# MLP input tiles and attention value rows transposed in 32x32 blocks on VectorE, regrouped through DRAM

## The reference

```
h = rmsnorm(x);  q, k, v, u, qx, gates = split(h @ w_in)
y_attn = windows of 128 keys over chunks of 64, 8 query heads, 2 kv heads of 64, with sinks
y_ssm  = glu(gelu(state space layer(u)));  y_mem = cross attention(qx, 256 memory rows)
merged = sum over branches of sigmoid(gate) * (y @ w_branch)
x = x + rmsnorm(merged @ w_out)
h2 = rmsnorm(x);  out = x + rmsnorm(relu(h2 @ w_up)**2 @ w_down)
```

## Time and profile before

| | |
|---|---|
| median of 3 runs | 1439.28 us (1438.74 to 1439.55) |
| profiled execution, its own time | 1438.89 us |
| its span, first to last instruction | 1436.9 us |
| mean granted clock | 0.998 |
| PE / PE weight load / DVE / ACT / POOL busy | 99% / 82% / 73% / 36% / 17% |
| PE's part of the chain that ended last | 94% |
| DMA | 227 MB, 158 GB/s over the span |

### The profile page before, as it was taken

One profiled execution on the slowest core, in us unless ns is written; L12 is line 12 of the kernel. 1 busy time (PEld: TensorE's weight loads), 2 busy tenths in 40 slices (PEclk: granted clock), 3 DMA queues, 4 the chain that ended last, 5 costly groups with the idle time before them and its releaser, 6 DMA issues.

```text
span 1436.9 us, 18375 instructions
## 1 busy us (share of the span) xinstructions
PE 1422.6 (99%) x6998; PEld 1178.1 (82%) x6998; DVE 1047.4 (73%) x1718; ACT 514.9 (36%) x637; POOL 241.7 (17%) x392
## 2 busy tenths in 40 slices
PE   8999999999999999999999999999999999999997
PEld 7888688878888888888888888888888888888886
DVE  6769768964854526456766779797979796979887
ACT  4445653131211352311333432333334333434334
POOL 0003313431111131001000304211010102020112
PEclk9999999999999999999999999999999999999999
DMA  9306525954234387234433447936363737364546
GB/s 337 74 30 190 166 85 175 275 195 149 71 106 139 93 272 256 93 96 151 162 104 89 133 146 228 299 118 203 119 203 117 234 94 239 105 203 143 160 152 117
DMA packets 136241, 227.04 MB, mean 158 GB/s; under 512 B 23048, under 2 KB 74288, under 8 KB 136176
## 3 DMA queue, kind: packets, MB, share of 16 engines
q0 software_dynamic: 52960, 139.24, 31.2%
q1 hardware_dynamic: 83200, 86.92, 19.1%
q10 hardware_dynamic: 16, 0.00, 0.0%
HBM read 175.53 MB, written 50.59 MB: 157 GB/s over the span
## 4 chain that ended last, share of the span: by engine, by line
PE 94%; DVE 3%; DMA 1%; issue 1%; ACT 0%; DVEq 0%; SPq 0%; ACTq 0%
PE bank L2146 55%; PE bank L2515 17%; PE bank L2535 15%; PE bank L2186 1%; PE bank L2156 1%; PE bank L2248 1%; PE bank L2268 1%; DMA raw<-in_w_down_dram 1%; PE bank L2375 1%; PE bank L2380 1%; PE bank L2284 1%; PE bank L2345 1%; PE bank L2330 1%; DMA xst<-in_mem_dram 0%; DVE wlo L388 0%
## 5 line engine op out<-in xcount | busy, mean ns | idle before, releaser
L2146 PE MATMUL bank<-hThi,whi 128*128 128x512 f32 x800 | 313.9, 392 | 0.1
L2146 PE MATMUL bank<-hThi,wlo 128*128 128x512 f32 x800 | 311.4, 389 | 0.0
L2146 PE MATMUL bank<-hTlo,whi 128*128 128x512 f32 x800 | 311.4, 389 | 0.0
L2146 PEld LDWEIGHTS bank<-hThi,whi 128*128 128x128 f32 x800 | 150.2, 188 | 32.2 <-issue 1.2
L2146 PEld LDWEIGHTS bank<-hThi,wlo 128*128 128x128 f32 x800 | 150.2, 188 | 31.6
L2146 PEld LDWEIGHTS bank<-hTlo,whi 128*128 128x128 f32 x800 | 150.2, 188 | 30.7
L1212 ACT ACTIVATE whi<-raw 128x1024 fp32r<-128x1024 f32 x91 | 95.3, 1055 | 182.3 <-DVE raw L1953 97.6
L1943 DVE TENSOR_TENSOR wlo<-raw,whi 128x1024 fp32r<-128x1024 f32 x91 | 110.9, 1219 | 34.4 <-ACT whi L1212 34.4
L2535 PE MATMUL bank<-whi,yhi 128*128 128x512 f32 x336 | 130.8, 389 | 0.6 <-DVE acc L1976 0.6
L2535 PE MATMUL bank<-wlo,yhi 128*128 128x512 f32 x336 | 130.7, 389 | 0.0
L2515 PE MATMUL bank<-hThi,whi 128*128 128x512 f32 x336 | 130.7, 389 | 0.0
(11 more groups left out here) (398 smaller groups left out, 2568.7 us busy)
## 6 DMA issues: line engine op xcount, KB each, us to landing
hThi<-h_scratch POOLq DMA_DIRECT2D x42, 512.0 KB, 4.8
hTlo<-h_scratch POOLq DMA_DIRECT2D x42, 512.0 KB, 5.7
raw<-in_w_in_dram SPq DMA_DIRECT2D x34, 512.0 KB, 7.2
raw<-in_w_up_dram SPq DMA_DIRECT2D x32, 512.0 KB, 4.3
raw<-in_w_down_dram SPq DMA_DIRECT2D x32, 512.0 KB, 4.6
gate_scratch<-scr POOLq DMA_DIRECT2D x48, 256.0 KB, 3.1
tok<-gate_scratch POOLq DMA_DIRECT2D x24, 512.0 KB, 4.2
prob_scratch<-pT POOLq DMA_DIRECT2D x16, 512.0 KB, 3.5
```

The costliest lines, as they stand in the source:

```text
L2146: ins = T.matmul(dst, lhs(k)[p], rhs(k)[q], start=start and k == 0 and i == 0, stop=stop and k == kt - 1 and i == 2)
```

## The change

- Attention: stage `vwin` is gone from PE and ACT. DVE transposes vT in 32x32 blocks right after `rope(7)`; POOL stores the result and, after the first gate unit, loads it back in four DMAs as `vwin` [128, 4, 16, 32]. `spv` issues 8 products of 256 columns per pair of chunks instead of 4, each 32 output channels wide, in four column groups.
- Output stage: for tiles 0 to 5, DVE transposes h2 in 32x32 blocks into acc[:, t] right after making it; POOL stores that (512 KB), waits for the store, and loads it back regrouped in four DMAs (128 KB each) over the same slot of `tok`. ACT and DVE make the high and low part from that slot in place of a bank. PE's 8 transposes per tile are gone for these tiles; before the MLP it waits for DVE's count of low parts. Tiles 6 and 7 stay as they were.
- `vwin` took 4 bank uses and h0 to h5 took 12, 16 in all, so the banks of all later uses are unchanged.

```
-OUT_ORDER stages: ("vwin", 4), ("out", 28)
+                  ("out", 16)
+HB = 6
...
+h2_slot = lambda t: tok[:, (2 + t % 2) * D:(3 + t % 2) * D]
+v_dram = nc.dram_tensor("v_blocks_scratch", (P, 2, NCH, 32), f32, kind="Internal").ap()
+hb_dram = nc.dram_tensor("h2_blocks_scratch", (HB, P, L), f32, kind="Internal").ap()
...
 # POOL, attention
+pool.wait_ge(blocks_turned, 9)
+g.dma_start(v_dram.rearrange("p b m r -> p (b m r)"), blocks[:, 0, :]).then_inc(blocks_out[0], 16)
 gates_out(0)
+pool.wait_ge(rope_done, 10)
+pool.wait_ge(blocks_out[0], 80)
+for b in range(4):
+    src = v_dram[:, b % 2, b // 2:b // 2 + 15, :].rearrange("(a s) m r -> s a (m r)", a=4)
+    g.dma_start(vwin[32 * b:32 * b + 32, :, 1:NCH, :].rearrange("s a m r -> s a (m r)"), src).then_inc(p_back, 16)
...
 # POOL, output stage, per tile t, behind the load of x
                     x_load(t + 2)
+                if t < HB:
+                    pool.wait_ge(blocks_turned, 17 + t + 1)
+                    g.dma_start(hb_dram[t], acc[:, t, :]).then_inc(blocks_out[t % 2], 16)
+                    pool.wait_ge(blocks_out[t % 2], 128 + 16 * (1 - t % 2) + 16 * (t // 2 + 1))
+                    src = hb_dram[t].rearrange("(a s) (b x) -> b s a x", a=4, b=4)
+                    for b in range(4):
+                        g.dma_start(h2_slot(t)[32 * b:32 * b + 32, :].rearrange("s (a x) -> s a x", a=4), src[b]).then_inc(xp_back[t % 2], 16)
...
 # ACT
-            for e in range(4):
-                copy_out(FIRST["vwin"] + e, vwin[:, 4 * e:4 * e + 4, :].rearrange("p n d -> p (n d)"))
...
             def h2_hi(t):
+                if t < HB:
+                    act.wait_ge(xp_back[t % 2], 16 * 16 + 64 * (t // 2 + 1))
+                    for e in range(2):
+                        A.activation(hThi[:, 4 * e:4 * e + 4, t * P:(t + 1) * P].rearrange("p k (a r) -> p k a r", a=4),
+                                     h2_slot(t).rearrange("p (a k r) -> p k a r", a=4, k=KT)[:, 4 * e:4 * e + 4], ACT.Copy).then_inc(split_hi, 1)
+                    return
...
 # DVE, after rope(7)
+            dve.wait_ge(blocks_out[0], 64)
+            V.transpose(blocks[:, 0, :].rearrange("p (b m r) -> p m b r", b=2, m=NCH),
+                        vT[:, :].rearrange("p (m b s) -> p m b s", m=NCH, b=2)).then_inc(blocks_turned, 1)
...
 # DVE, residual(t) and h2(t)
+                if 4 <= t < HB + 4:
+                    dve.wait_ge(blocks_out[t % 2], 128 + 16 * (1 - t % 2) + 16 * (t // 2 - 1))
...
+                if t < HB:
+                    dve.wait_ge(h2_made, t + 1)
+                    V.transpose(acc[:, t, :].rearrange("p (b k r) -> p k b r", b=4, k=KT),
+                                h2_slot(t).rearrange("p (k b s) -> p k b s", k=KT, b=4)).then_inc(blocks_turned, 1)
...
 # DVE, h2_lo(t)
+                if t < HB:
+                    for e in range(2):
+                        by_block = lambda y: y[:, 4 * e:4 * e + 4, t * P:(t + 1) * P].rearrange("p k (a r) -> p k a r", a=4)
+                        dve.wait_ge(split_hi, 20 + 2 * t + e + 1)
+                        V.tensor_tensor(by_block(hTlo), h2_slot(t).rearrange("p (a k r) -> p k a r", a=4, k=KT)[:, 4 * e:4 * e + 4],
+                                        by_block(hThi).bitcast(f32), sub).then_inc(h_parts, 1)
+                    return
...
 # PE
-            for e in range(4):
-                starts = [max(0, 64 * (4 * e + i - 1)) for i in range(4)]
-                transposes(FIRST["vwin"] + e, [vT[:, s0:s0 + P] for s0 in starts])
...
-                    for j in range(2):
-                        t0 = 4 * j + 2 * nn
+                    for a4 in (0, 2, 1, 3):
+                        t0 = 4 * (a4 // 2) + 2 * nn
...
                 if step[0] == "h":
-                    h2_transposes(t)
+                    if t >= HB:
+                        h2_transposes(t)
...
-            for t in range(4):
-                for e in range(2):
-                    wait_taken(pe, out_event("h", t, e))
+            pe.wait_ge(h_parts, 8)
```

More of the change, by code:

```diff
@@ L42 @@
 U_GATE = [9, 12, 13] + list(range(14, 23))
-STAGES = [("front", 26), ("qx", 12), ("spar", 1), ("xsc", 16), ("q", 8), ("kv", 4), ("xpv", 8), ("ssc0", 8), ("g0", 4), ("vwin", 4),
[1 row of a table removed]
+STAGES = [("front", 26), ("qx", 12), ("spar", 1), ("xsc", 16), ("q", 8), ("kv", 4), ("xpv", 8), ("ssc0", 8), ("g0", 4),           ("ssc1", 8), ("u", 8), ("g1", 4), ("g2", 4), ("spc", 2), ("spv", 8), ("s5a0", 2), ("g3", 4),
           ("s5m0", 2), ("g4", 4), ("s5y0", 2), ("s5a1", 2), ("g5", 4), ("s5m1", 2), ("g6", 4), ("s5y1", 2), ("s5a2", 2),
           ("g7", 4), ("s5m2", 2), ("g8", 4), ("s5y2", 2), ("s5a3", 2), ("g9", 4), ("s5m3", 2), ("g10", 4), ("s5y3", 2), ("g11", 4), ("mergeA", 16),
-          ("glu", 16), ("mergeM", 16), ("mergeS", 16), ("out", 28), ("upA", 4), ("mlp", 192)]
+          ("glu", 16), ("mergeM", 16), ("mergeS", 16), ("out", 16), ("upA", 4), ("mlp", 192)]
 OUT_ORDER = ["w0", "w1", "w2", "h0", "w3", "h1", "w4", "h2", "w5", "h3", "w6", "h4", "w7", "h5", "h6", "h7"]
+HB = 6
+OUT_EVENTS = [w for w in OUT_ORDER if w[0] == "w" or int(w[1]) >= HB]
 FIRST = {}
@@ L136, in out_event @@
         return FIRST["upA"] + 2 + 3 * (t - 6) + e
-    return FIRST["out"] + 2 * OUT_ORDER.index(f"{kind}{t}") + e
+    return FIRST["out"] + 2 * OUT_EVENTS.index(f"{kind}{t}") + e
 UP_FIRST = [(0, 0, 0), (0, 1, 0), (1, 0, 0), (1, 1, 0), (0, 0, 1), (0, 1, 1), (1, 0, 1), (1, 1, 1)]
@@ L228, in hybrid_layer @@
                 with overlay() as ov2:
-                    vwin = ov2("vwin", [P, NCH, P])
+                    vwin = ov2("vwin", [P, 4, NCH, 32])
         with overlay() as ov:
@@ L315, in hybrid_layer @@
         x_turned, x_out, x_back_in = sem("x_turned"), sem("x_out"), sem("x_back_in")
+        h_parts = sem("h_parts")
         blocks_turned, blocks_out, p_back = sem("blocks_turned"), [sem(f"blocks_out{s}") for s in range(2)], sem("p_back")
@@ L708, in blocks_back @@
             def blocks_back(q):
[L710 removed]
+                pool.wait_ge(blocks_out[q % 2], 64 + 16 * (1 - q % 2) + 16 * (q // 2 + 1))
                 src = p_dram[q].rearrange("(a s) (b x) -> b s a x", a=4, b=4)
@@ L715, in _ @@
             for q in range(8):
-                pool.wait_ge(blocks_turned, 8 + q + 1)
+                pool.wait_ge(blocks_turned, 9 + q + 1)
                 g.dma_start(p_dram[q], blocks[:, q % 2, :]).then_inc(blocks_out[q % 2], 16)
@@ L1546, in _ @@
             rope(7)
+            for e in range(2, 4):
+                wait_taken(dve, FIRST["kv"] + e)
+            dve.wait_ge(blocks_out[0], 64)
+            V.transpose(blocks[:, 0, :].rearrange("p (b m r) -> p m b r", b=2, m=NCH),
+                        vT[:, :].rearrange("p (m b s) -> p m b s", m=NCH, b=2)).then_inc(blocks_turned, 1)
             SS = float(HD) ** -0.5
@@ L1651, in _ @@
             for h in range(2):
-                dve.wait_ge(blocks_out[h], 128)
+                dve.wait_ge(blocks_out[h], 144 - 16 * h)
             temps = (t1, t2, t3, t4)
@@ L1839, in h2 @@
                 dve.wait_ge(sq_x, t + 1)
-                if t >= 2:
+                if 2 <= t < HB + 2:
+                    dve.wait_ge(h_parts, 2 * (t - 1))
+                elif t >= 2:
                     wait_full(dve, out_event("h", t - 2, 0))
@@ L2318, in _ @@
                 transposes(FIRST["spc"] + ri, [craw[:, ri, r, :, :].rearrange("p d x -> p (d x)") for r in range(4)])
-            for e in range(4):
-                wait_taken(pe, FIRST["vwin"] + e)
-            pe.wait_ge(p_back, 16 * 4 * 8)
+            pe.wait_ge(p_back, 16 * 4 * 9)
             for q in range(8):
@@ L2327, in _ @@
                     nk = 64 if q == 0 and nn == 0 else P
-                    for j in range(2):
-                        t0 = 4 * j + 2 * nn
-                        ins = T.matmul(banks[n % 8][64 * j:64 * j + 64, nn * 256:nn * 256 + 256].rearrange("p (t a r) -> p t a r", t=2, a=4),
-                                       vwin[0:nk, 2 * q + nn, 64 * j:64 * j + 64], turned_p[0:nk, t0:t0 + 2, :, :],
+                    for a4 in (0, 2, 1, 3):
+                        t0 = 4 * (a4 // 2) + 2 * nn
+                        ins = T.matmul(banks[n % 8][32 * a4:32 * a4 + 32, nn * 256:nn * 256 + 256].rearrange("p (t a r) -> p t a r", t=2, a=4),
+                                       vwin[0:nk, a4, max(1, 2 * q + nn), :], turned_p[0:nk, t0:t0 + 2, :, :],
                                        start=True, stop=True)
@@ L2474, in plain_mlp @@
                     if pc == 4:
-                        for t in range(4, NT):
+                        if HB > 4:
+                            pe.wait_ge(h_parts, 2 * HB)
+                        for t in range(HB, NT):
                             for e in range(2):
```

4 lines of the change are left out of this document (1 added, 3 removed), and 1 row of the table STAGES.

## The result

The changed kernel takes 1448.28 us (median of 4 runs, 1446.92 to 1449.30) against 1439.41 us (1438.74 to 1439.95) for the kernel before on the same chip: ratio 1.0062, 95% interval 1.0048 to 1.0077. The forecast was 1444.9 us, range 1435.5 to 1452, slower with a chance of 0.63. The direction and the place were right, and so was the mechanism as far as it went; the size fell short by 3.4 us.

The account below looks back on a forecast made before the run. PE, busy for 99% of the span, was taken to bound the kernel. 1438.89 - 7.0 (transposes) + 10.8 (stall) + 1.8 (clock) = 1444.5 us, 1444.9 on the median's scale, range 1435.5 to 1452.

Parts of the forecast that it names:

- What comes off: PE's transposes removed: 1.75 us for vwin and 5.2 us for six h2 tiles, together 7.0 us saved.
- The value products: Attention on PE: 64 products in four column groups take as long as before, bounds -0.1 and +0.6 us.
- The rest of attention: DVE's 1.25 us transpose fits its 9.35 us of idle time, and POOL's added DMAs delay nothing: cost zero.
- POOL's round: Output stage: POOL waits for two store landings per tile, so its round takes 12.6 us against PE's 10.9.
- The stall of 10.8 us: Before the first up-projection product, PE waits 10.8 us for weights' parts standing behind tile 4's late return from DRAM.
- POOL keeps pace: Rival: stores in POOL's queue land in 2.9 us, round 8.7 us, PE waits only 2.0 us; 1434.3 us, chance 0.17.
- The floor of 2.0 us: Before the first up-projection product, PE's wait from DVE's order alone if POOL keeps pace: 2.0 us.
- The clock: The stall lowers PE's granted clock, and the restart costs 1.8 us more, bounds 0 and 4.
- The waits behind the stall: Other waits in the output stage and MLP, such as for h6's and h7's transposes, add nothing.
- late next, with 1.5 us to spare: PE's transposes of h6 and h7 would bind next, through the same POOL rounds, if the stall were shorter.
- crowded queues: Rival: block loads take some 3 us longer each round in the output stage, adding 15 us: 1460 us, chance 0.04.
- The sum: Whole kernel: 1438.89 - 7.0 + 10.8 + 1.8 = 1444.5 us for the profiled execution, 1444.9 on the median's scale.

Follow-up runs that it names:

- e_values: Changed kernel with only the value rows through DVE and DRAM, all eight MLP input tiles transposed on PE as before: 1437.96 us, ratio 0.9986.
- e_deep_order: e_deep_sp with DVE making the first weights' low part before tile 5's transpose, and tiles 6 and 7's parts earlier: 1433.17 us, ratio 0.9950.
- e_sp_queue: Changed kernel with the block stores and loads of the six tiles issued from SP's queue instead of POOL's: 1444.41 us, ratio 1.0031.
- e_x1_first: Changed kernel with POOL issuing the next tile's x1 store before it waits for the block store: 1440.12 us, ratio 1.0004.
- e_deep: Changed kernel with blocks loaded back into acc[:, t], each h step one tile later, weights' parts ahead of tile 4's: 1444.02 us, ratio 1.0025.
- e_x1_weights: e_x1_first with the first up weights' parts made before tile 4's parts on ACT and DVE: 1438.41 us, ratio 0.9996.
- e_deep_x1: e_deep with POOL issuing the next tile's x1 store before it waits for the block store: 1436.04 us, ratio 0.9965.
- e_deep_sp: e_deep with the block stores and loads in SP's queue: 1434.27 us, ratio 0.9963.
- e_weights_first: Changed kernel with the first up weights' parts made before tile 4's parts on ACT and DVE: 1447.89 us, ratio 1.0057.

## Why the prediction came out as it did

*What comes off, 7.0 us: right.* Stretch A lost 1.77 us (forecast 1.75), in the changed kernel and in e_values alone. The other 5.2 us show in e_deep_order, where little hides them.

*The value products, no change with bounds -0.1 and +0.6: right,* 7.2 us in both traces. The rest of attention cost nothing that can be seen: DVE's idle time of 9.35 us shrank to 8.15, which is the transpose's 1.2 us.

*POOL's round, 12.6 us: right in sum.* It was 12.7. The block store was waited for until 5.6 us after its issue (forecast 5.3 and 0.1 for the wait), the x1 store until 4.0 us (forecast 4.4 and 0.1), the four loads took 2.2. Four of the five rounds are 11.9 to 13.1 us, 12.4 in the mean; the first is 13.85, because its block store goes out behind DVE's transpose and is waited for longer (6.04 us of idle time). The prediction gave every round the same length, and weighed it against the Trainium skill, page "DMA: Bandwidth & Descriptors", section "Anatomy of one DMA — SWDGE (gpsimd) path", whose fit of 2.0 us plus the bytes at 436 GB/s gives an estimated 3.2 us for 512 KB. The trace does not agree for a store behind a load: the block stores landed 5.3 us after their issue here.

*The stall of 10.8 us: mechanism and place right, size short by 1.5.* The working gave 805.3 - 794.2 = 11.1 and rounded it down; PE waited 12.28. The missing 1.2 us are 0.7 in the rounds (51.1 us for four, not 50.4) and some 0.4 in tile 4's own trip. What the prediction told as one cause has more, though. Its working follows POOL's round, and that is what binds in the changed kernel: from its second round on, POOL idles for its own stores and not for another engine (one idle time of 4.05 us is put down to "issue"). In e_sp_queue that round is gone and PE still waits 10.35 us for the trip, but its trip is longer than the changed kernel's, with two tiles in 25.1 us. In e_x1_first, with POOL at 10.8 us per round and a store of 4.9 us, the same two tiles take 785.21 - 762.69 = 22.5 us against PE's 21.8, and PE waits 5.14 us. What the trip alone would keep in the changed kernel was not measured; these two kernels give 10.35 and 5.14 us. Most of the 5.14 us is no excess of a loop either: it is the 9.6 us of tile 4's own trip, with the weights' parts behind it. e_deep shows that with the trip out of the chain the round alone keeps 8.80 us. The delays run side by side, and only the kernels that shorten the round and move the trip give the gain. Of e_deep's three changes none was tried alone with a short round, except the weights' place (e_x1_weights, 1438.41 us); so that the free slot and the extra tile of time are both needed is argued from DVE's order, not shown.

The rival "POOL keeps pace" was said to be decided by a round under 10.9 us, and that was wrong: in e_x1_first the round is 10.8 us, and the time was 1440.12 and not the rival's 1434.3. The rival's own condition, stores that land in 2.9 us, was met nowhere. The floor of 2.0 us was near: 1.83 us in e_deep_x1 and e_deep_sp, once nothing else was late, though the steps of DVE stand in another order there.

*The clock, 1.8 us: the size came out, and as far as the record goes by luck.* The row of 805 to 810 gives 1.8. But the prediction took its 1.8 from the 16 first transposes of the kernel, 3.9 us in place of 2.1, and over them the trace of the kernel before shows a granted clock of 1.00 (the stretch below). What lengthened them is not shown, so that row is no price of a lowered clock:

```profile
4.50:8.50 4.00, 3.85 (x16) 3.14 (x16) 2.08 (x3) 2.29 (x4) 0.00 (x0) 1.00 1.07 395
```

*The waits behind the stall, put at nothing: wrong, and this is the step that failed.* What the prediction says of the transposes of h6 and h7, "late next, with 1.5 us to spare", held: they did not wait here, and h7's did (0.90 us) in e_weights_first, where the stall is shorter. But it looked only at these transposes and not at the low parts behind them. PE waited another 1.63 us at 833, for tile 7's low part. DVE makes it behind tile 5's, and ACT's high part of tile 5 waited 10.99 us for its blocks: their four loads landed after 6.6 us and not 2.9. The issues by DMA of the stretch from 800 to 815 say what was in flight beside them:

```profile
raw<-in_w_down_dram SPq DMA_DIRECT2D x4, 512.0 KB, 6.5
out_dram<-yst POOLq DMA_DIRECT2D x2, 512.0 KB, 8.9
...
tok<-h_blocks_scratch POOLq DMA_DIRECT2D x4, 128.0 KB, 6.6
```

The prediction had looked for SP's loads in 730 to 798 us and found none, which is true, and had not asked what tile 5's trip meets after 805, when the released weight unit lets four loads of w_down go. That is its "crowded queues" rival, for one tile. e_sp_queue speaks for it: there the w_down loads are queued behind tile 5's, and ACT starts on tile 5 at 807.58, 4.2 us after its loads began to be issued; here it was 11.6 us (807.37 to 818.97).

*The sum.* The execution shown took 4.8 us more than 1444.5. The start gave 1.0. Stretch B grew by 10.79 us where the forecast's terms add up to 7.4 (-5.2 + 10.8 + 1.8): 1.5 us of the difference are the stall, 1.6 the second wait, and 0.3 are not settled. The last 0.4 us lie behind stretch B and stay open.

## What to carry to other kernels

Before a helper trip is hung into a pipeline, write down every loop that it closes, each queue's round and each buffer's way from one fill to the next, and compare each with the step of the bounding engine; a loop that is longer costs its excess times the number of tiles, and shortening one of two such loops shows only what the other leaves. Then look at the last trip: what has to wait for it, and what stands behind it on the same engine, is late by its whole length even where no loop is too long. What worked here was a buffer for the trip that is dead anyway, together with one more step of distance for its consumer and a shorter round of the queue. Moving a late result behind other work only moves the stall.

## What was not expected of the hardware

A short wait can cost the clock, and the same wait need not. e_deep_x1 and e_deep_sp both have a gap of 1.83 us before the first up product. In the first the granted clock fell behind it towards its lower level (0.5, 1.2 GHz), in the second it did not (stretches, columns as above; first e_deep_x1, then e_deep_sp):

```profile
796.00:798.00 2.00, 2.00 (x7) 1.50 (x6) 2.00 (x2) 1.49 (x4) 0.97 (x2) 0.52 0.97 258
798.00:800.00 2.00, 2.00 (x7) 1.62 (x6) 1.76 (x10) 0.00 (x0) 1.24 (x3) 0.63 0.82 232
```
```profile
796.00:798.00 2.00, 2.00 (x11) 1.65 (x10) 1.86 (x8) 0.27 (x1) 0.00 (x0) 1.00 0.38 117
798.00:800.00 2.00, 2.00 (x11) 1.65 (x10) 1.86 (x5) 0.00 (x0) 0.00 (x0) 1.00 0.85 261
```

The counts are of products that touch the stretch, 7 in place of 11; from 796.3 to 799.3 us each took 0.43 us in place of 0.23. The seven executions of e_deep_x1 fall into two groups by their mean granted clock: 1433.6 to 1434.7 us at 0.998, and 1436.0 to 1436.5 at 0.996. So a stall of 2 us was worth 2 us or 4 there, and nothing tried says what decides it. In e_deep_sp, one execution of five stands at 0.996 (1435.51 us), but its slowest, 1436.86 us, is at 0.999, so the clock is not all of the spread. In e_deep_order, with 0.58 us, all five stand at 0.998 or above. That the clock is the cause of the two groups is read from their clocks, not tried by itself.

The same block store of 512 KB landed at different times from kernel to kernel (medians): 5.3 us in the changed kernel, alone behind an x load of its queue; 4.8 us in e_deep_x1, with the x1 store issued behind it; 6.4 and 6.8 us from SP's queue with an x load and an x1 store in POOL's (e_deep_sp, e_sp_queue). How much of that is the queue and how much the company was not tried apart.
